# Memory attention in one decoder layer: four decode sequences at a time on 32-column groups, and the last query lengths inside the attention block

## The reference, cut to what matters

```python
def memory_attend(hn, mem_k, mem_v, lw):
    B, T, _ = hn.shape
    q = rmsnorm((hn @ lw['w_mq']).reshape(B, T, MEM_HEADS, MEM_HD), lw['mem_q_norm_g'])
    s = jnp.einsum('bqhd,bkhd->bhqk', q, mem_k.astype(q.dtype), preferred_element_type=jnp.float32) * (MEM_HD ** -0.5)
    p = jax.nn.softmax(s, axis=-1).astype(hn.dtype)
    o = jnp.einsum('bhqk,bkhd->bqhd', p, mem_v.astype(hn.dtype)).reshape(B, T, D_MODEL)
    return o @ lw['w_mo']
```

## Time and profile before

| | |
|---|---|
| Median of 3 runs | 1862.36 us (1858.97 to 1865.31) |
| The profiled execution's own time | 1858.68 us |
| Its span, first to last instruction | 1857.4 us |
| TensorE busy | 1785.0 us, 96% |
| VectorE / ScalarE / GpSimd busy | 63% / 42% / 40% |
| DMA engines, mean | 101 GB/s over the span |

### The profile page before, as it was taken

One profiled execution on the slowest core, in us unless ns is written; L12 is line 12 of the kernel. 1 busy time (PEld: TensorE's weight loads), 2 busy tenths in 40 slices (PEclk: granted clock), 3 DMA queues, 4 the chain that ended last, 5 costly groups with the idle time before them and its releaser, 6 DMA issues. The chain is left out here.

```text
span 1857.4 us, 27758 instructions
## 1 busy us (share of the span) xinstructions
PE 1785.0 (96%) x10347; PEld 1626.3 (88%) x10347; DVE 1168.7 (63%) x1377; ACT 780.6 (42%) x1488; POOL 741.6 (40%) x637
## 2 busy tenths in 40 slices
PE   6999999989989999998999989999999999999999
PEld 5999999989967787997777879999999999987787
DVE  6335655856676623423425268888788888699985
ACT  5015673325675432312134254444444444444432
POOL 4001221015544340211116117766666666457643
PEclk9999999999989999999999999999999999999999
DMA  5122112242254320113522221222222222596554
GB/s 172 49 59 62 36 36 70 64 124 80 64 153 162 118 109 27 44 67 136 182 80 91 68 76 60 80 74 71 71 71 71 71 71 71 175 346 212 159 172 149
DMA packets 159289, 188.06 MB, mean 101 GB/s; under 512 B 14065, under 2 KB 112986, under 8 KB 158776
## 3 DMA queue, kind: packets, MB, share of 16 engines
q1 hardware_dynamic: 158280, 186.55, 30.8%
q0 software_dynamic: 896, 0.19, 0.1%
q10 hardware_dynamic: 16, 0.00, 0.0%
HBM read 151.64 MB, written 35.07 MB: 101 GB/s over the span
## 5 line engine op out<-in xcount | busy, mean ns | idle before, releaser
L3724 PE MATMUL ffn_banks<-h_parts,up_hi 128*128 128x384 f32 x1920 | 489.3, 335 | 8.8 <-DVE h_parts L4222 5.5
L3724 PEld LDWEIGHTS ffn_banks<-h_parts,up_hi 128*128 128x128 f32 x1920 | 346.0, 188 | 11.3 <-issue 8.9
L3724 PE MATMUL ffn_banks<-h_parts,up_lo 128*128 128x384 f32 x960 | 321.3, 335 | 0.0
L4121 POOL TENSOR_TENSOR up_lo<-up_raw,up_hi 128x512 fp32r<-128x512 f32 x174 | 261.4, 1519 | 132.8 <-ACT up_hi L3886 88.4
L987 PE MATMUL proj_banks<-x_hi,in_w_hi 128*128 128x384 f32 x624 | 214.9, 344 | 0.5 <-DVE x_lo L251 0.5
L987 PE MATMUL proj_banks<-x_hi,in_w_lo 128*128 128x384 f32 x624 | 208.8, 335 | 0.0
L987 PE MATMUL proj_banks<-x_lo,in_w_hi 128*128 128x384 f32 x624 | 208.6, 334 | 0.0
L3724 PEld LDWEIGHTS ffn_banks<-h_parts,up_lo 128*128 128x128 f32 x960 | 180.6, 188 | 0.0
L4166 POOL TENSOR_TENSOR h_parts<-down_cells,h_parts 128x512 fp32r<-128x512 f32 x69 | 110.7, 1613 | 90.0 <-ACT h_parts L3959 90.0
L3845 PE MATMUL ffn_banks<-h_parts,up_hi 128*128 128x512 f32 x352 | 138.2, 393 | 2.8 <-DVE h L4394 1.4
L3848 PE MATMUL ffn_banks<-h_parts,up_lo 128*128 128x512 f32 x352 | 137.1, 390 | 0.0
(11 more groups left out here) (551 smaller groups left out, 3829.4 us busy)
## 6 DMA issues: line engine op xcount, KB each, us to landing
up_raw<-in_w_up SPq DMA_DIRECT2D x44, 512.0 KB, 3.9
down_cells<-in_w_down SPq DMA_DIRECT2D x58, 256.0 KB, 5.1
up_raw<-ffn_gated_rows SPq DMA_DIRECT2D x44, 320.0 KB, 5.2
ffn_gated_rows<-h SPq DMA_DIRECT2D x22, 576.0 KB, 2.8
in_w_raw<-in_w_in SPq DMA_DIRECT2D x24, 512.0 KB, 3.9
up_raw<-ffn_gated_rows SPq DMA_DIRECT2D x44, 256.0 KB, 3.3
spill<-mixT SPq DMA_DIRECT2D x10, 576.0 KB, 3.9
h_kept<-h SPq DMA_DIRECT2D x9, 512.0 KB, 2.6
```

The lines of the kernel that those rows point to most:

```text
L3724: ins = nc.tensor.matmul(banks[:, bank, 0:TC], wt[:, j, k, :], parts[:, q, x, k, :], start=(fresh and n == 1), stop=(n == last), skip_grou ...
L4121: nc.gpsimd.tensor_tensor(w_lo[:, j], weights.full(j), w_hi[:, j].bitcast(F32), ALU.subtract).then_inc(weights.split[j], 1)
```

## The change

1. Decode sequences are handled in sets of four (`SETS` = 2, `X` = 4): set g holds sequences g, g + 2, g + 4, g + 6, each on 32 columns of its own. `HEAD_STEPS` becomes 8, `EARLY` becomes 1. A set's score step has 8 products with 32 columns of weights, and stands between the turning of the next step's sequences 0, 1 and 2, 3.
2. The turned keys of odd steps lie in `attnT` (the trace's `mem_attn_t`) at tiles 4 and 5, which are written last. Two more cache slots (6 and 7) lie in `attnT` at tiles 1, 2, 3 and last, with pieces of 128 elements. So all eight sequences' keys have a place, and SP issues them at once; the values of slots 0 to 3 wait for set 0's turned keys, those of slots 4 to 7 for set 1's.
3. The masks: one copy for each set, in columns that are the same for queries and probabilities, so that nothing is cleared in between.
4. The chain behind the last query tile moves into the attention block: the last squares are VectorE's first instruction there, `sum_squares` stands between heads 1 and 2 of score(0), `turn_sums` behind score(0), copy and root are ScalarE's first instructions, reciprocal and factor stand behind the first maximum.
5. `output(3)` waits for its own last product before it frees the values.

```diff
@@ query_projection @@
-            sum_squares(n_tiles - 1)
-            turn_sums()
...
-            act.wait_ge(summed, n_tiles // 2 + 1)
-            nc.scalar.activation(squares[0:32 * NP, 0, 0:TC], more[0:32 * NP, 0:TC], ACT.Copy).then_inc(rows_copied, 1)
-            act.wait_ge(rows_turned, 1)
...
-            for n in range(n_tiles):
+            for n in range(n_tiles - 1):
...
-            dve.wait_ge(rooted, 1)
-            nc.vector.reciprocal(inv_norm[:], root[:]).then_inc(inverted, 1)
-            dve.wait_ge(inverted, 1)
@@ memory_attention @@
+        SETS, X = 2, 4
+        HEAD_STEPS, EARLY = HEADS * SETS, 1
...
+        keys_at = [k_one_t[:], attnT[:, :, 4 * P:6 * P]]
+        free_tiles = [attnT[:, :, P * t:P * t + P] for t in (1, 2, 3, last)]
...
         def cols(x):
-            return slice(64 * x, 64 * x + 64)
+            return slice(32 * x, 32 * x + 32)
...
+            for slot in range(NB):
+                load("cache_mem_k", slot)
+            for slot in range(NB):
+                if slot % X == 0:
+                    sp.wait_ge(k_turned, X * HEADS * (slot // X + 1))
+                load("cache_mem_v", slot)
+            sp.wait_ge(v_used, 1)
             next_weights.load_first(sp)
...
-            def turn_keys(n):
+            def turn_keys(n, xs):
...
-                for x in range(2):
+                for x in xs:
+                    slot, m = X * g + x, X * n + x
                     if h == 0:
-                        wait_landed(pe, K_SLOT[g], x, K_USE[g])
-                    if n:
-                        pe.wait_ge(k_copied, 2 * (n - 1) + x + 1)
-                    if n == EARLY:
+                        wait_landed(pe, slot, 1)
+                    if m >= 2:
+                        pe.wait_ge(k_copied, m - 1)
+                    if n == EARLY and x == 0:
                         pe.wait_ge(out_copied, SAMPLE_AT - 2)
...
                 pe.wait_ge(masked_ready, g + 1)
-                pe.wait_ge(k_copied, 2 * n + 2)
+                pe.wait_ge(k_copied, X * n + X)
                 for j in range(2):
-                    for x in range(2):
+                    for x in range(X):
...
-                for n in range(1, HEAD_STEPS):
-                    if n >= EARLY:
-                        turn_keys(n)
-                    pair_scores(out, n - 1)
-                pair_scores(out, HEAD_STEPS - 1)
+                for n in range(EARLY, HEAD_STEPS):
+                    turn_keys(n, (0, 1))
+                    set_scores(out, n - 1)
+                    turn_keys(n, (2, 3))
+                set_scores(out, HEAD_STEPS - 1)
...
                 for h in range(HEADS):
+                    if i == 0 and h == 2:
+                        sum_squares()
...
                     ins.then_inc(valued, 1)
+                    pe.wait_ge(valued, i + 1)
+                    pe.sem_inc(v_used, 1)
                     return
...
             score(0)
+            turn_sums()
             score(1)
             for n in range(EARLY):
-                turn_keys(n)
+                turn_keys(n, range(X))
...
+                if i == 0:
+                    dve.wait_ge(rooted, 1)
+                    nc.vector.reciprocal(inv_norm[:], root[:]).then_inc(lengths_inverted, 1)
+                    dve.wait_ge(lengths_inverted, 1)
+                    nc.vector.tensor_scalar(factor[:], inv_norm[:], 1.0 / 16, None, ALU.mult).then_inc(factored, 1)
+                    dve.wait_ge(factored, 1)
...
+            nc.vector.tensor_tensor(squares[:, 1, :], qT[:, KD - 1, :], qT[:, KD - 1, :], ALU.mult).then_inc(squared, 1)
             maxima(0)
...
-            for i in range(SAMPLE_AT):
+            for g in range(SETS):
+                mask(g, qT[:, :, TP:T])
+            for i in range(SAMPLE_AT + 2):
                 normalize(i)
```

More of the change, by code:

```diff
@@ L2913, in sum_squares @@
                     ins = nc.tensor.matmul(more[32 * p:32 * p + 32, 0:TC], head_col, squares[:, n % 2, TC * p:TC * p + TC],
-                                           start=(n == 1), stop=(n == n_tiles - 1), skip_group_check=True)
+                                           start=(n == 1), stop=False, skip_group_check=True)
                 ins.then_inc(summed, 1)
[L2917 to L2922, removed]
             pe.wait_ge(w_high_half, 1)
@@ L3054, in cols, with wait_landed @@
+        def wait_landed(engine, slot, use):
+            engine.wait_ge(landed[slot], 32 * use)
         def cols(x):
-            return slice(64 * x, 64 * x + 64)
+            return slice(32 * x, 32 * x + 32)
         @block.sync
         def _(sp):
-            def load(g, name, slot):
-                for x in range(2):
-                    for kt in range(2):
-                        sp.dma_start(cache(slot, x, kt), A[name][0, g + PAIRS * x, P * kt:P * kt + P].rearrange("p h d -> p (h d)")
-                                     ).then_inc(landed[slot][x], 16)
@@ L3065, in _, with load @@
[L3065 to L3075, removed]
+            def load(name, slot):
+                g, x = divmod(slot, X)
+                for kt in range(2):
+                    frm = A[name][0, SETS * x + g, P * kt:P * kt + P].rearrange("p h d -> p (h d)")
+                    if slot >= 6:
+                        frm = frm.rearrange("p (f c) -> p f c", c=P)
+                    sp.dma_start(cache(slot, kt), frm).then_inc(landed[slot], 16)
@@ L3108, in sample_scores, with sum_squares, turn_sums @@
             def sample_scores(out):
[L3110 to L3114 removed]
+                for n in range(EARLY, HEAD_STEPS):
[3 more added lines that the diff above has]
+                set_scores(out, HEAD_STEPS - 1)
                 pe.wait_ge(k_used, HEAD_STEPS)
                 pe.sem_inc(scored, 1)
+            def sum_squares():
+                pe.wait_ge(squared, 1)
+                for g in range(NP):
+                    ins = nc.tensor.matmul(more[32 * g:32 * g + 32, 0:TC], one_col[:, 0:32], squares[:, 1, TC * g:TC * g + TC],
+                                           start=False, stop=True, skip_group_check=True)
+                ins.then_inc(summed, 1)
+            def turn_sums():
+                pe.wait_ge(sums_copied, 1)
+                for j in range(NP):
+                    ins = nc.tensor.transpose(sums[:, j, :], squares[0:32 * NP, 0, P * j:P * j + P], C.ident[0:32 * NP, 0:32 * NP])
+                ins.then_inc(sums_turned, 1)
             def score(i):
@@ L3272, in exponentials @@
                                          ).then_inc(exp_done, 1)
+            act.wait_ge(summed, 1)
+            nc.scalar.activation(squares[0:32 * NP, 0, 0:TC], more[0:32 * NP, 0:TC], ACT.Copy).then_inc(sums_copied, 1)
+            act.wait_ge(sums_turned, 1)
+            by_tile = sums[:].rearrange("q j (g c) -> q g j c", g=NP)[:, :, :, 0:HEADS]
+            nc.scalar.activation(root[:].rearrange("q (g j) c -> q g j c", g=NP), by_tile, ACT.Sqrt, scale=1.0 / 256,
+                                 bias=C.eps[:, 0:1]).then_inc(rooted, 1)
             act.wait_ge(factored, 1)
```

119 lines of the change are left out of this document (52 added, 67 removed).

## The result

The changed kernel takes 1848.59 us (median of 6, 1846.71 to 1852.35) against 1862.94 us (6 runs of before, 1858.97 to 1865.31): ratio 0.9931, 95% interval 0.9919 to 0.9943. The forecast was 1849. Its profiled execution has a span of 1846.7 us, 10.7 less than before's; the medians lie 14.4 apart. The two differences disagree by 3.7 us mainly because before's profiled execution lies 4.3 us under its median and this one's (1848.32 us) 0.3 us under.

What follows compares the result with a forecast made beforehand. TensorE, busy 96% of the span, was taken to bound the kernel. 3.8 + 0 - 1.7 + 2.9 + 8.1 = 13.1 us gained: 1845.6 by the profiled execution, 1849 beside the median; range 1843 to 1857.

Steps and rivals of the forecast that it cites:

- A: Chain behind the query tiles: the attention block, and every start in it, comes 3.8 us earlier.
- B: Attention block's start to turn(0): 0 us, the wait for GpSimd replaced by an equally long one for DMA.
- D: Decode tile's scores: period 3.6 us in place of 4.08, stage 28.2 against 31.0; 2.9 us gained.
- E: Decode tile's output: 64 products in 16 rounds of four, 7.0 us, no late values; 8.1 us gained.
- C: TensorE's clock falls to half in the wait for key loads at the attention block's start; 1.7 us lost.
- rival that took 3.07: Four column groups run only 3.07 times as fast, a round 0.56 us, not 0.44: 1853 us; chance 0.07.
- what is won before 980.5 should be carried to the end: After 980.5 TensorE is busy 805.75 of 819.50 us, so no earlier gain should be lost there.
- pairs of groups: Rival: no more than two small groups work together in decode scores and output; sum -0.7, 1863 us; chance 0.05.
- late values: Rival: set 1's values miss 47.7 us in the decode output, say 8 us late: 1857 us; chance 0.04.
- a slow clock in the loop: Rival: clock falls and stays at half in the decode score loop; 1864 us, or 1887 with later stages; chance 0.03.
- a kernel with no wait and no fall: Rival: no key-load wait before turn(0), 1.5 us gained, and no clock loss: 1846 us; chance 0.10.
- Given back: Rival: a later stage hangs on a store or load that does not move; up to 13 us, 1862; chance 0.05.

Runs made afterwards that it cites:

- the chain alone: Kernel before with only the last query lengths' chain moved into the attention block (two banks allocated in the new order): 1857.8 us, 0.9983 of before.
- the run with four places: Changed kernel with four places for turned keys, not two, and all 16 transposes of a step ahead of its score step: 1842.34 us, 0.9904 of before.
- score(2) in the wait: Changed kernel with score(2) moved ahead of the third and fourth sequence's early transposes: 1848.14 us, 0.9933 of the kernel before.
- sets of four alone: Changed kernel with the chain of the last query lengths put back at the end of the query block: 1853.85 us, 0.9965 of the kernel before.

## Why the prediction was right, point by point

The forecast of 1849 met 1848.59, and part of that is luck. By the profiled executions, which its sum was made against, it said 1845.6 and 1848.32 came: the stages give 10.5 us where the sum has 13.1. The rest of the agreement is that the medians lie 14.4 apart and the traces 10.7. The terms A, B, D and E hold each by itself; C was too small, and a loss behind the attention was missing.

- **A** was 4.05, not 3.8: a block end cost 0.5 us behind VectorE's reciprocal, but only 0.3 behind TensorE's sum. The doubt on the squares came out at 0.
- **B** was right to 0.1 us, and for the reason given: the fourth sequence's keys replaced GpSimd's normalizing as the last to come. But two errors cancel in the 0.1: these transposes started at 13.9 us, not 14.4, and took 0.91 us at half clock, not 0.44. In the other traces of this form turn(0) stands at 15.0 to 15.4 us. That without this wait 1.6 us more could be had is shown by the chain alone (B 13.2).
- **C** was the term mis-sized: 2.5 us against 1.7. The step that failed is "half of a little more is lost", with 3.1 us for the stretch: by its row it lasted 6.8 us, turn(0) and most of score(2) lay in it, some 4.9 of their 6.86 us, and half of that was lost. That the wait causes it is shown by filling the wait. Its length is not fixed (C 5.3 to 6.9 us in five traces), so 1.7 lies within what single traces show and 2.5 at the upper end. The row set against a fall (2.10 us of work in 4.75 at 1.00) was weak evidence, as the chain alone showed.
- **D** was 2.8 against 2.9 (31.0 less 28.2, as worked out there, is 2.8 too), period 3.62 against 3.6. Both parts of the reading hold: the score step takes as long for four sequences as for two, and 0.7 us of each period went in the run with four places, where TensorE no longer waits for VectorE.
- **E** was 8.1 as forecast; some 7 of it come from 16 rounds of four in place of 32 of two, the rest from waits that are gone. The bound for the last values has a slip (four loads at 1.25 us and four at 3.9 are 20.6 us, not 22), on the safe side: no load was waited for. 64 products take 6.9 us; one after another they would take 64 x 0.433 = 27.7, an estimate from the full-array product. That is four times. The Trainium skill, page "TensorE: Matmul & The Clock Gate", section "Measured speedup vs the span model", has 3.07 for four row groups and 2.38 for three column groups, and none for four column groups. The forecast's rival that took 3.07 for them did not happen: back to back the four column groups give the full factor here.
- **Not foreseen**: 2.0 us behind the attention. The step "what is won before 980.5 should be carried to the end" failed by that much. The changed kernel's clock is 0.62 from 967.9 to 972.3, where the kernel before passed the same pause (977.8 to 980.5) at full clock; from the first product with w_mo to the feed-forward part's first it takes 104.3 us in place of 102.9. It is no accident of one execution. Of the eight traces with both parts of the change, seven take 104.2 to 104.3 us; the eighth (score(2) in the wait), either part alone and the kernel before take 102.9 to 103.0. So neither part brings it by itself. What TensorE did in the 20 us before the first product with w_mo does not tell them apart: it was busy 8.8 of 10.0, 2.2 of 3.4, 3.8 of 3.9 and 0.0 of 2.7 us in both. What decides stays open; it costs 1.3 us. The remaining 0.7 us lies within what the feed-forward part varies by between these traces (773.8 to 775.7).
- **The rivals**: pairs of groups and late values did not happen, nor did a slow clock in the loop (granted clock 1.00 from 877.0 to 904.4, TensorE busy 23.80 of 27.40 us), nor a kernel with no wait and no fall. "Given back" happened in small, 2.0 us, but by the clock and the feed-forward part's spread, with no store or load named.

## What to carry to other kernels

Small products on column groups are worth filling up to four, but the time won shows only as far as the step around them can move: look at how many places the feeding transposes have, and how often TensorE changes between the two kinds. When a stage starts earlier, ask which load it now meets; and where TensorE must wait for one, put real work there (here the next tile's scores), because waits like the two of 1.9 us here cost their own length and then 0.9 to 2.5 us more by the half clock. Shorter ones did not always: with sets of four alone TensorE stood 1.33 and 0.99 us and the clock stayed at 1.00.

## What the runs showed of the hardware that was not expected

- A score step with the groups in the order 0, 0, 1, 1, 2, 2, 3, 3 took 1.02 us against 1.00 for 0, 1, 2, 3, 0, 1, 2, 3: neighbours on one group did not hold up the others.
- 5.25 us of work in 6.00 kept the clock, where 0.77 in 3.80 lost it; adding useless products brought output(0) 2.0 us forward, in one trace.
- The same pause of 2.7 us ahead of w_mo's first product was followed by 4.4 us at a granted clock of 1.00 in four traces and of 0.61 to 0.64 in seven, with the same work before it.
- A run of 8 or 16 records on 32 columns behind transposes took 0.13 to 0.14 us more than its rounds of 0.433 us (0.57 for 0.43, 1.00 for 0.87), and eight transposes behind such a run took 1.03 where eight ahead of full-array products took 0.87.
